# Opening of a two-block transformer kernel: the products of the first two weight units in another order

## The reference

```python
h = rmsnorm(x, g_mix[l])
z = jnp.einsum('bsd,dc->bsc', h, w_in[l])
cb, cc, cv, q, k, v, f_logit, gate_c, gate_a = jnp.split(z, SPLIT_POINTS, axis=-1)
...
gc = jax.nn.sigmoid(gate_c + b_gate[l, :D_MODEL])
ga = jax.nn.sigmoid(gate_a + b_gate[l, D_MODEL:])
```

## Time and profile before

| | us |
|---|---|
| median of 3 runs | 2414.88 |
| lowest and highest run | 2413.97 and 2416.67 |
| the profiled execution, its own time | 2415.09 |
| its span in the trace | 2413.3 |
| PE busy in it | 2388.2 (99%) |
| DVE busy in it | 1971.6 (82%) |
| ACT busy in it | 1262.8 (52%) |

### The profile page before, as it was taken

One profiled execution on the slowest core, in us unless ns is written; L12 is line 12 of the kernel. 1 busy time (PEld: TensorE's weight loads), 2 busy tenths in 40 slices (PEclk: granted clock), 3 DMA queues, 4 the chain that ended last, 5 costly groups with the idle time before them and its releaser, 6 DMA issues.

```text
span 2413.3 us, 47723 instructions
## 1 busy us (share of the span) xinstructions
PE 2388.2 (99%) x14373; PEld 2142.2 (89%) x14373; DVE 1971.6 (82%) x3176; ACT 1262.8 (52%) x2038; POOL 88.4 (4%) x109
## 2 busy tenths in 40 slices
PE   8999999999999999999999999999999999999998
PEld 7898898999899999999998888889898999999997
DVE  7778876689998887887899877776887887887886
ACT  6444445566554454554555555565544545445455
POOL 0000001000000000000000015300000000000000
PEclk9999999999999999999999999999999999999999
DMA  7886885657888888888888555555466656656555
GB/s 273 282 288 210 283 289 194 201 194 262 293 299 298 293 297 296 290 297 296 294 295 274 183 182 194 190 169 196 159 195 191 210 185 202 201 183 214 196 177 171
DMA packets 162812, 566.81 MB, mean 235 GB/s; under 512 B 18883, under 2 KB 19452, under 8 KB 162748
## 3 DMA queue, kind: packets, MB, share of 16 engines
q1 hardware_dynamic: 132572, 458.71, 56.6%
q10 hardware_dynamic: 27792, 101.20, 12.7%
q0 software_dynamic: 2384, 6.09, 1.0%
HBM read 563.51 MB, written 2.42 MB: 235 GB/s over the span
## 4 chain that ended last, share of the span: by engine, by line
PE 73%; DVE 6%; issue 3%; ACT 1%; DVEq 1%; DMA 1%; ACTq 0%; POOL 0%; SPq 0%; POOLq 0%
PE bank L339 73%; DVE w_lo L1356 2%; DVE ada_w L1375 1%; DVE scratch L1362 1%; DVE H L1341 1%; DVE scratch L2003 0%; DVE scratch L2001 0%; ACT w_hi L828 0%; DMA ada_w<-in_w_ada 0%; DVE scratch L2006 0%; DMA w_raw<-in_w_in 0%; DVE Z L1714 0%; DVE scratch L2029 0%; ACT U L1302 0%; DVE ss L1615 0%
## 5 line engine op out<-in xcount | busy, mean ns | idle before, releaser
L1356 DVE TENSOR_TENSOR w_lo<-w_raw,w_hi 128x1024 fp32r<-128x1024 f32 (+2 forms) x898 | 1047.4, 1175 | 112.9 <-ACT w_hi L828 103.1
L339 PE MATMUL bank<-H,w_hi 128*128 128x512 f32 (+1 forms) x4480 | 1080.6, 380 | 12.3 <-ACT w_hi L280 8.1
L339 PEld LDWEIGHTS bank<-H,w_hi 128*128 128x128 f32 x4480 | 799.0, 188 | 127.3 <-issue 11.9
L828 ACT ACTIVATE w_hi<-w_raw 128x1024 fp32r<-128x1024 f32 (+2 forms) x898 | 877.0, 1011 | 25.1 <-DMA w_raw<-in_w_up 7.5
L339 PEld LDWEIGHTS bank<-H,w_lo 128*128 128x128 f32 x4416 | 586.9, 188 | 36.0 <-DVE w_lo L1356 1.1
L339 PE MATMUL bank<-H,w_lo 128*128 128x256 f32 x4416 | 596.8, 275 | 0.1
L339 PE MATMUL bank<-U,w_hi 128*128 128x512 f32 (+1 forms) x2011 | 492.5, 378 | 1.0 <-DVE U L2031 0.7
L858 ACT ACTIVATE scratch<-bank 128x256 f32<-128x256 f32 x355 | 135.0, 380 | 628.4 <-PE bank L339 627.6
L339 PEld LDWEIGHTS bank<-U,w_hi 128*128 128x128 f32 x2011 | 351.5, 188 | 44.7 <-DVE U L2031 1.0
L339 PEld LDWEIGHTS bank<-U,w_lo 128*128 128x128 f32 x1984 | 274.2, 188 | 20.5
L339 PE MATMUL bank<-U,w_lo 128*128 128x256 f32 x1984 | 280.0, 275 | 0.0
(11 more groups left out here) (245 smaller groups left out, 1119.4 us busy)
## 6 DMA issues: line engine op xcount, KB each, us to landing
w_raw<-in_w_ff SPq DMA_DIRECT2D x256, 512.0 KB, 5.2
ada_w<-in_w_ada ACTq DMA_DIRECT2D x192, 512.0 KB, 4.7
w_raw<-in_w_up SPq DMA_DIRECT2D x176, 512.0 KB, 4.6
w_raw<-in_w_z SPq DMA_DIRECT2D x96, 512.0 KB, 4.9
w_raw<-in_w_in SPq DMA_DIRECT2D x88, 512.0 KB, 4.4
w_raw<-in_w_gate SPq DMA_DIRECT2D x64, 512.0 KB, 4.6
w_raw<-in_w_down SPq DMA_DIRECT2D x64, 384.0 KB, 3.1
w_raw<-in_w_down SPq DMA_DIRECT2D x64, 320.0 KB, 3.4
```

What stands on the lines that cost most here:

```text
L339: return nc.tensor.matmul(out, lhsT, rhs, start=start, stop=stop, skip_group_check=True)
L828: A(w_hi[:, slot, 0:cols], w_raw[:, slot, 0:cols], ACT.Copy).then_inc(sem("w_high"), 1)
L1356: TT(w_lo[:, slot, 0:cols], w_raw[:, slot, 0:cols], w_hi[:, slot, 0:cols].bitcast(F32), ALU.subtract)\
```

## The change

In the opening, with the slots in the order 0, 2, 1, 3 (`FIRST_ORDER`) for loads and casts:

- PE makes the long products of slot 0, then those of slot 2 (the other unit), the short ones of slot 0, the long ones of slots 1 and 3, and then the short ones of slots 1, 2 and 3. The long products of unit 0 wait for one chunk at a time.
- SP loads a quarter of x and a piece in turns: x0, slot 0, x1, slot 2, x2, slot 1, x3, slot 3.
- ACT makes a quarter of the high parts and a cast in turns, the casts in the same order.
- DVE makes the low parts of chunks 0 to 7, the split of slot 0, chunks 8 to 15, and then the splits of slots 1, 2 and 3.

Nothing is computed more or less often, and everything behind the first pair stands as it was.

```diff
+FIRST_ORDER = [0, 2, 1, 3]
...
             for i in range(4):
                 sp.dma_start(X[:, 4 * i:4 * i + 4, :], t["x"][:, 4 * i:4 * i + 4, :]).then_inc(sem("x_landed%d" % i), 16)
-                if i < 2:
-                    piece(sp, 0, i, t["w_gate"], 0, first=True)
-            for s in (2, 3):
-                piece(sp, 0, s, t["w_gate"], 0, first=True)
+                piece(sp, 0, FIRST_ORDER[i], t["w_gate"], 0, first=True)
...
-            pair_of_units(PAIR0["gate"], H, NC, "h_ready", CHUNKS["h1"])
+            def highs_of_first(par, h):
+
+                pe.wait_ge(sem("w_high"), FIRST_ORDER.index(2 * par + h) + 1)
+                for c in range(FIRST_CHUNKS):
+                    k = FIRST_CHUNKS * h + c
+                    if par == 0:
+                        pe.wait_ge(sem("h_ready"), k + 1)
+                    mm_lines(bank[par][:, :], w_hi[:, 2 * par + h, c * P:(c + 1) * P], whole(H, k), k == 0, False)
+
+            def lows_of_first(par, h):
+
+                pe.wait_ge(sem("w_split"), CREDIT + 2 * par + h + 1)
+                for c in range(FIRST_CHUNKS):
+                    k = FIRST_CHUNKS * h + c
+                    end = mm_lines(bank[par][:, T:2 * T], w_lo[:, 2 * par + h, c * P:(c + 1) * P], ob(H, k, 0), False, k == NC - 1)
+                end.then_inc(sem("piece_used"), 1)
+
+            pe.wait_ge(sem("bank_read"), 2)
+            highs_of_first(0, 0)
+            highs_of_first(1, 0)
+            lows_of_first(0, 0)
+            highs_of_first(0, 1)
+            highs_of_first(1, 1)
+            lows_of_first(0, 1)
+            lows_of_first(1, 0)
+            lows_of_first(1, 1)
             pair_of_units(PAIR0["gate"] + 1, H, NC)
...
             for i in range(4):
                 first_chunks(i)
-                if i < 2:
-                    cast_high0(act, A, i)
-            cast_high0(act, A, 2)
-            cast_high0(act, A, 3)
+                cast_high0(act, A, FIRST_ORDER[i])
...
             def first_low(i):
-                dve.wait_ge(sem("w_high"), i + 1)
+                dve.wait_ge(sem("w_high"), FIRST_ORDER.index(i) + 1)
                 TT(w_lo[:, i, :], w_raw[:, i, :], w_hi[:, i, :].bitcast(F32), ALU.subtract).then_inc(sem("w_split"), 1)
...
-                if i < 2:
-                    first_low(i)
-            first_low(2)
-            first_low(3)
+                if i == 1:
+                    first_low(0)
+            for i in range(1, 4):
+                first_low(i)
```

## The result

| | median us | lowest to highest | runs |
|---|---|---|---|
| before | 2414.52 | 2413.82 to 2417.60 | 22 |
| changed | 2418.10 | 2416.57 to 2420.78 | 22 |

The ratio is 1.0015, 95% interval 1.0009 to 1.0021: the change costs 3.6 us. By the bound of 0.2% named with the prediction this is "same", but it is clearly slower than before, it is four times the 0.9 us that were forecast, and it lies just outside the range.

A forecast was written before the change was run, and what follows sets the result against it. PE, busy 99% of the span, was taken as the bound. The first pair's 2.2 us gain is lost waiting for `ss`, +0.9 us net: 2415.09 becomes 2416.0 profiled, 2415.8 as median; range 2413.8 to 2418.0.

The forecast's parts named there:

- The mechanism: Opening to norm: 2.2 us won in the first pair, wholly given back because slot 1's next piece is issued later.
- the chain of 13 us: From pair 1's cast of slot 1 on ACT to the end of `ss` on DVE: 13.28 us, moving with the piece's landing.
- the 2.2 us that PE was to win: First pair on PE: ends at 21.4 instead of 23.55, and pair 1 at 32.0 instead of 34.2.
- The term: Product with `ss` on PE: starts at 35.05 instead of 34.22, with some 0.1 to refill, +0.9 us.
- that on the loads: Opening loads: x3 lands at 13.6, hidden by 0.3; the first four pieces only change places; cost nothing.
- the cover of 0.3 us: Ahead of chunk 12: ACT's high part is ready at 14.1 and DVE asks for it at 14.4.
- The row behind the 3.8: Load time of pair 1's slot 1 piece: 3.8 us, from the issue at 18.02, taken as an almost empty queue.
- The clock's fall: Rival: behind PE's new wait the clock drops to 1.2 GHz, 1.7 us more, 2417.5 in all; chance 0.13.
- the idle of 1.46 us: At 640.54, before the change: eight long products after it took 2.12 us, full pace; cited against the clock rival.
- the forecast's own upper end: Slot 1's piece takes 4.9 us to load: +2.0 us, 2416.9.
- The place near 1324 us: Earlier trace's clock fall to 1.2 GHz, read as following only one-column products and short waits; 1.7 us lost.
- No gain from the piece in time: Even with slot 1's piece there in time, ACT copies unit 0's half bank at 19.7 and `ss` comes at 34.3.

The follow-up runs named there:

- e4: Kernel before with only DVE's new order (split 0 behind chunk 7, splits 1 to 3 behind chunk 15): 2415.94 us, ratio 1.0005.
- e1: Changed kernel with the sum of squares moved behind the first unit of the third pair: 2412.96 us, ratio 0.9993.
- e2: Changed kernel with six unused products of ones with x's first chunk put ahead of the sum of squares: 2415.87 us, ratio 1.0006.
- e10: Kernel before with a PE wait for ACT's last cast for the third pair put ahead of the sum of squares: 2418.80 us, ratio 1.0015.
- e11: e10 with five unused products of ones with x's first chunk ahead of the same wait: 2417.06 us, ratio 1.0011.
- e3: Changed kernel with the split of slot 1 behind chunk 11 instead of behind chunk 15: 2416.93 us, ratio 1.0007.
- e9: e3 with unit 0's second run of short products ahead of unit 1's second run of long ones: 2414.66 us, ratio 1.0000.

## Why the prediction was wrong

- **The mechanism was right.** The gain of the first pair was given back at the norm because the piece for slot 1 is issued behind its late split; ACT's wait for the DMA, the chain of 13 us and PE's wait for `ss` stand where the prediction put them. e4 shows the split alone doing it, e1 that without the wait nothing is lost. That the idle measured 2.92 us, with 3.0 forecast, is luck: pair 1 ended at 33.3 instead of 32.0 and `ss` at 36.06 instead of 35.0, so both ends were late by about as much. Of the 2.2 us that PE was to win, 1.3 stood at the end of the first pair and 1.1 at the end of the second.
- **The term was mis-sized: +2.0 us instead of +0.9.** The piece was issued at 18.64, not 17.88 (0.76), it took 4.28 us, not 3.8 (0.48), and the chain was 0.17 shorter; together 1.07. The step that failed is that on the loads: "The first four pieces change places only, and each cast still comes before PE needs it. Cost nothing." In e1 and e2, with the same loads and splits as the changed kernel, x3 lands at 14.3 to 14.4 us instead of 13.6, the cover of 0.3 us is used up, DVE waits 0.25 and 0.37 us ahead of chunk 12 (the row below is e2's), and the splits start at 17.0 instead of 16.5. That is 0.5 of the 0.76. The rest is in the trace of the changed kernel alone: there chunks 4 to 7 start at 9.56 instead of 9.05 (9.09 in e2), because slot 0's piece and x1, which are issued ahead of the moved piece, landed late, as they did in e10 with the loads of before.

```profile
14.89 2.19 DVE L1363 SCALAR_TENSOR_TENSOR H<-X,vec,H 128x128 fp32r<-128x128 f32 x8 [0.37 <-ACT H L902]
```

- **The load's own time** of 4.28 us lies inside the ends that were kept, and e4's piece took 4.6. The row behind the 3.8 was not one of an almost empty queue: at 18.02 two pieces were still to land, at 19.3 and 20.6. The Trainium skill's fit ("DMA: Bandwidth & Descriptors", the anatomy of a DMA), an estimate of 3.2 us, is further off.
- **A rival came on top of the forecast.** The clock's fall was priced rightly (1.7 us forecast, 1.65 in the trace, 1.7 between the medians of e10 and e11) but given 0.13 and left out of the sum, with the idle of 1.46 us that did not bring it down as the ground. That row is half as long as the idle that the forecast itself contained; it said nothing on 3 us. The warning in the Trainium skill ("TensorE: Matmul & The Clock Gate", why this matters for kernels) agrees with these runs in kind, but the gap that it names is longer than the idles of 2.04 and 2.41 us after which the clock fell here, and the measurement decides; the fall should have been the likelier case. With the forecast's own upper end (2416.9) it gives 2418.6, which the range should have held; it ended at 2418.0. The place near 1324 us was misread in part: ahead of it stand not only products of one column, but six of 256 to 512 columns among them.
- **No gain from the piece in time: right, for the reason given.** The prediction had unit 0's copy on ACT as the next limit, at 19.7, with `ss` at 34.3; e3 ran into it at 21.06, with `ss` at 35.39.
- Of the 3.7 us that PE is behind at 41.48, the profiled execution shows 3.0 at its end (2418.08 against 2415.09). One later wait is seen to be shorter, that before 640.54 with 1.12 us instead of 1.46; the rest was not followed.

## What to carry to other kernels

Where an engine makes products ahead of time, follow what its *results* release: buffers, loads and side sums keep the old order, and the next wait in program order takes the gain back. Price the idle that a reordering creates twice, once as time and once as the clock that can fall behind it, and either move work into it or move the waiting instruction back. Here moving one sum behind the next unit took away the whole loss of 3.6 us; by the medians 1.6 us are won (e1_sum_later, 2412.96), which its interval doesn't separate from nothing.

## What the runs showed of the hardware

- After PE idles of 0.75 (e4), 1.04 (e9) and 1.46 us the granted clock held; after 2.04 (e3), 2.41 (e10) and 2.92 us (the changed kernel) it went to 1.2 GHz in the profiled executions, 0.1 us (e3) to 1.7 us (e10) after the products had begun again. How long it stays down differs: in e3's trace the windows from 36 to 42 us all show 0.50, in the changed kernel's only that from 38 to 40.
- The same instructions do not always bring the clock down. The times of e10 suggest a fall in about two executions of three. The fall near 1324 us stands in the traces of before, changed and nine of the ten experiments, but e11's shows 1.00 in every window from 1316 to 1332 us, this one among them:

```profile
1326.00:1328.00 2.00, 1.43 (x8) 1.05 (x9) 1.89 (x5) 1.38 (x4) 1.10 (x2) 1.00 0.08 31
```

- With slot 2's piece as the second weight load, the input `w_dt` landed between 18.75 and 18.97 us in six kernels; with slot 1's it landed between 18.01 and 18.05 in five and at 18.47 in the sixth, e10, where slot 0's piece was already 0.7 us late. In five of the six the second piece itself took 0.6 to 0.8 us longer behind x1. What makes the difference was not tried.
